# Token projections: the inverse norms go onto a diagonal that TensorE multiplies by

## The chip, the core and the metric

The program runs on one core of a Trainium2 chip. The metric is the device time of one execution in microseconds, as the median of three runs. TensorE (PE in the rows) does the matmuls, with PEld for its weight loads; VectorE is DVE, ScalarE is ACT, GpSimd is POOL and SyncE is SP.

## The reference, cut to what matters

The reference is two model blocks of two layers each, in float32. Every layer ends its mixer and its feed-forward part with the same step: a projection from a wide activation to the 1024 model columns, a root-mean-square norm over these columns, and a gated addition to the residual. Cut down, with `hidden` tokens by features:

```
m = hidden @ w_down                                   # (tokens, 1024)
n = m * rsqrt(mean(m * m, axis=-1) + 1e-6)            # one factor per token
h = h + n * gain                                      # gain: one factor per model column
```

There are 256 context tokens and 256 latent tokens in the first layer of the first block, 256 latent tokens after it.

## The kernel before, in words

The residual `h` and nearly all activations lie with model columns on the partitions (eight tiles of 128 columns, `KT`) and tokens along the free dimension (`S` = 256 for one half). Eight projections are computed the other way round, by the class `TokenProjection` (L897): 128 tokens on the partitions, 512 model columns in a bank. Each handles 256 tokens by 1024 columns as a two by two block scheme with seven products instead of eight (L971, `product`), all products in float32. The seven bank sums are combined by VectorE (`combine`, L1040) into four quarters `y[:, q]` of 128 tokens by 512 columns: q = 0 and 1 are the two column halves of tokens 0 to 127 (half 0), q = 2 and 3 those of tokens 128 to 255 (half 1).

Because tokens are on the partitions, the norm is one number per partition. ScalarE squares each quarter with a running sum along the row (L1029) and takes the root (L1034); VectorE takes the reciprocal (L1065). Half 1 is ready first. Then the quarters are scaled in place by the reciprocals: 2, 3 and 0 by VectorE (L1068), 1 by ScalarE (L1036). TensorE turns the scaled quarters back (`turn`, L1010): for half 1 and then half 0, eight transposes of 128x128 against the identity, from `y` into two banks' halves. VectorE adds them to the residual with the gain (`residual`, L1070, one instruction per k, L1075), waiting for the transposes of a pair of k in half 0.

The eight projections stand in these places:

- Projection A and projection B, the two token halves of the first layer's down projection (`WideDown`, L1181). B's products are interleaved with the end of A: A's transposes are in four groups, each between products of B (L1225). B's own transposes come after eight key products of `ContextKeys` (L1117).
- The output projections of the second layer of block one and of both layers of block two, and the down projections of the same three layers. `run` (L1077) issues products, then all 16 transposes. After five of the seven projections other than A (B, and those whose tails are at 1202, 1433, 1585 and 1991 us) `modulated_norm` (L555) follows: ScalarE squares each residual tile (L484), TensorE sums by a product with ones (L502), ScalarE takes the root (L489), VectorE the reciprocal (L510) and the normed tiles (L566). After the other two (1804 and 2211 us) a projection by the gate matrix follows directly on the residual tiles (L414).

The order of work on each engine is that of the program text: each stage adds its part to the queue of each engine, and the parts run in the order in which they were added, with semaphores between engines (`hit` names a count, `need` waits for it). Weights come through a ring of five chunks that SyncE's queue refills (L3051) when the products that read a chunk are done. Nothing plans or reorders. `K.root` is a scratch tile of two rows of 512 columns; its row 0 is used by the norms, its row 1 for a running sum of squares in other stages.

Of the kernel before, what the change touches and what calls it, by code (L numbers as in the profile page):

```python
# [16 lines left out]
ALU = mybir.AluOpType  # L17
ACT = mybir.ActivationFunctionType
AX = mybir.AxisListType.X

P = 128
D = 1024
KT = D // P
# [263 lines left out]
def need(eng, deps):  # L287

    for sig, count in deps:
        if count > 0:  # L290
            eng.wait_ge(sig.sem, count)
# [170 lines left out]


def scale_stage(K, groups, T, lhs, scale, apply, deps, eps="eps", n_apply=None, src_ready=None, sums=None):


# [8 lines left out]
    def scalar(act):  # L475
        need(act, deps)
        i = 0 if sums is None else 1
        for g, tiles in enumerate(groups):
            for t, src in enumerate(tiles if sums is None else []):
                if src_ready:  # L480
                    need(act, src_ready(t))
                if i >= n_square:
                    act.wait_ge(summed.sem, su + i - n_square + 1)
                act.activation(square[:, i % n_square, 0:T], src, ACT.Square).then_inc(squared.sem, 1)  # L484
                i += 1
            act.wait_ge(summed.sem, su + i)
            if g >= 2:
                act.wait_ge(applied.sem, ap + (g - 1) * (n_apply or len(groups)) // len(groups))
            act.activation(K.root[:, g % 2, 0:T], K.bank(4 + g % 2, T), ACT.Sqrt, bias=K.c(eps), scale=scale).then_inc(rooted.sem, 1)  # L489
# [119 lines left out]
class Modulation:  # L609
# [30 lines left out]
    def turn(self, pe):  # L640
        need(pe, self.after(1))
        for m in range(4):
            mm = pe.transpose(self.K.bank(self.banks[1])[:, m * P:m * P + P], self.row[:, m * P:m * P + P], self.K.c("ident"))
        mm.then_inc(self.sig[2].sem, 1)
# [9 lines left out]
def first_norm(K, h, piece, gains, gain, shift, out, tokens_ready, rest_of_constants):  # L654
# [17 lines left out]
    def scalar(act):  # L672
        need(act, tokens_ready)
        for k in range(KT):
            act.activation(out[:, k, :], h[:, k, :], ACT.Square).then_inc(sg["squared"].sem, 1)
        act.wait_ge(sg["summed"].sem, at["summed"] + 1)
        act.activation(r, K.bank(5), ACT.Sqrt, bias=K.c("eps"), scale=1.0 / D).then_inc(sg["rooted"].sem, 1)
        piece.keep(act)
        rest_of_constants(act)
        act.wait_ge(sg["n_gains"].sem, at["n_gains"] + 1)  # L680
        for k in range(1, KT, 2):
            act.wait_ge(sg["n_unit"].sem, at["n_unit"] + k + 1)
            for x, scale, bias in halves(k):
                ins = act.activation(x, x, ACT.Identity, bias=bias, scale=scale)
            ins.then_inc(sg["n_by_scalar"].sem, 1)
# [45 lines left out]
def attention_stage(K, rounds, outs, deps, buf, beside=None):  # L731
# [28 lines left out]
    def tensor(pe):  # L760
# [48 lines left out]
        for r in range(len(rounds) + 2):  # L809
            if r < len(rounds):  # L810
                score(r)
            if 1 <= r <= len(rounds):
                turn(r - 1)
                spread_inverse(r - 1)
            if r >= 2:
                weigh(r - 2)
# [80 lines left out]
class TokenProjection:  # L897
# [27 lines left out]
            K.next_blocks(CB, (self.sg["f_products"], self.at["f_products"] + (p + 1 if p < n - 2 else n + 5)))  # L925

    def reserve_tail(self):
        counts = {"squared": 4, "summed": 1, "rooted": 2, "row_inverses": 2, "taken_out_by_vector": 3, "taken_out_by_scalar": 1, "turned": KT, "applied": KT}
        self.sg.update({c: self.K.counter(c) for c in counts})
        self.at.update({c: self.sg[c].reserve(x) for c, x in counts.items()})  # L930

# [76 lines left out]
            self.product(pe, n - 1, i).then_inc(self.sg["f_products"].sem, 1)  # L1008

    def turn(self, pe, tiles):  # L1010
        scaled = {2: ("taken_out_by_vector", 1), 3: ("taken_out_by_vector", 2), 0: ("taken_out_by_vector", 3), 1: ("taken_out_by_scalar", 1)}
        for half in (1, 0):
            for k in tiles:
                if k % 4 == 0 or k == tiles[0]:
                    need(pe, [self.hit(*scaled[2 * half + k // 4])])
                mm = pe.transpose(self.tile(k)[:, half * P:half * P + P], self.y[:, 2 * half + k // 4, k % 4 * P:k % 4 * P + P], self.K.c("ident"))
                if not half:
                    mm.then_inc(self.sg["turned"].sem, 1)

    def norm(self, act):  # L1020
        sg, y = self.sg, self.y
        sums, partial, root, inverse = self.K.token_sum, self.K.token_partial, self.K.token_root[:, 0:2], self.K.token_inverse[:, 0:2]
        need(act, [self.final(1)])
        act.activation(y[:, 0], self.bank[1], ACT.Copy).then_inc(sg["f_first"].sem, 1)  # L1024
        for j, q in enumerate((0, 3, 2, 1)):
            need(act, [self.hit("f_quarters", j + 1)])
            if j == 2:
                need(act, [self.hit("squared", 1)])
            act.activation(self.junk[:, j % 2], y[:, q], ACT.Square, accum_out=sums[:, q:q + 1]).then_inc(sg["squared"].sem, 1)  # L1029
            if j >= 2:  # L1030
                half = 3 - j
                need(act, [self.hit("summed", 1)])
                need(act, [self.hit("squared", j + 1)])
                act.activation(root[:, half:half + 1], sums[:, q:q + 1], ACT.Sqrt, bias=partial[:, half:half + 1], scale=1.0 / D).then_inc(sg["rooted"].sem, 1)  # L1034
        need(act, [self.hit("row_inverses", 2)])
        act.activation(y[:, 1], y[:, 1], ACT.Copy, scale=inverse[:, 0:1]).then_inc(sg["taken_out_by_scalar"].sem, 1)  # L1036

    def combine(self, dve):
        sg, y, bank = self.sg, self.y, self.bank
# [19 lines left out]
    def scale(self, dve):  # L1059
        sg, y = self.sg, self.y  # L1060
        root, inverse = self.K.token_root[:, 0:2], self.K.token_inverse[:, 0:2]
        for half in (1, 0):
            iv = inverse[:, half:half + 1]
            need(dve, [self.hit("rooted", 2 - half)])
            dve.reciprocal(iv, root[:, half:half + 1]).then_inc(sg["row_inverses"].sem, 1)  # L1065
            need(dve, [self.hit("row_inverses", 2 - half)])
            for q in (2, 3) if half else (0,):
                dve.tensor_scalar(y[:, q], y[:, q], iv, None, ALU.mult).then_inc(sg["taken_out_by_vector"].sem, 1)  # L1068

    def residual(self, dve, h, gain, tiles):  # L1070
        lo = self.half * S
# [783 lines left out]
def even_projections(K, R, u, k_ready, qkvT, gate, qd, kvd, kpe, ktok, vtok, pads, conv, narrow, low_squares):  # L1855
# [24 lines left out]
    def tensor(pe):  # L1880
# [66 lines left out]
        for f in range(NF - 1):  # L1947
            project(f)
            if f == 1:
                key_rows()  # L1950
            elif f == 2:
                cumulate()
            if 3 <= f <= 10:
                unit_sum(f - 3)
            if f == 14 or f == 15:
                turn(2 * f - 28)
                turn(2 * f - 27)
            if f == 15:
                low_rank(0)
                low_rank(1)  # L1960
            if f == 16:
                for i in range(4, 8):
                    turn(i)
# [1144 lines left out]
```

## Time and profile before

| | us |
|---|---|
| median of three runs | 2255.86 |
| lowest, highest | 2252.78, 2255.88 |
| profiled execution, own time | 2256.64 |
| its span, first to last instruction | 2254.8 |
| TensorE matmul busy | 2171.7 (96%) |
| VectorE busy | 1051.4 (47%) |
| ScalarE busy | 461.0 (20%) |

The span is what the trace covers; the own time has a little more around it. The mean granted TensorE clock is 0.99 of full speed. Shares of busy time are means over the whole program.

### The profile page before, as it was taken

Reading aid. Unit: us, or ns where it says so; the run is one execution under the profiler, and the core shown is the slowest. Engines: PE = TensorE matmul, PEld = TensorE weight load, DVE = VectorE, ACT = ScalarE, POOL = GpSimd, SP = SyncE. Lnnn points to the kernel's source line nnn. Section 1 sums busy time; section 2 is a strip of 40 time slices with the busy share of each in tenths; the row PEclk is TensorE's granted clock in tenths of the full one; section 3 lists DMA queues with packets and bytes.
Section 4 is the critical chain, followed back from the end, with each engine's and each line's share of the span. In section 5 each row is a group of like instructions: output and inputs, shape, how many; then the busy total and the mean of one; then the engine's idle time right before and its main releaser. Section 6 shows DMA issues by size and latency. Waiting matters only on the chain.

```text
span 2254.8 us, 33258 instructions
## 1 busy us (share of the span) xinstructions
PE 2171.7 (96%) x14252; PEld 1512.5 (67%) x14252; DVE 1051.4 (47%) x1884; ACT 461.0 (20%) x988; POOL 139.0 (6%) x148
## 2 busy tenths in 40 slices
PE   6999999899899999999998999999999999999998
PEld 3447878464588885457466885686785478768646
DVE  2665555461654456652344114585324428642443
ACT  2433211351200000022153000223210022311001
POOL 0004333000000000002100000002000000200000
PEclk9999999999899999999999999999999999999999
DMA  8221444402422223445103444333344443334442
GB/s 324 75 75 43 152 154 167 160 1 75 187 94 79 90 94 132 173 147 141 60 1 131 149 150 169 142 128 113 126 154 168 150 149 114 111 131 149 168 168 75
DMA packets 41088, 285.66 MB, mean 127 GB/s; under 512 B 4976, under 2 KB 6384, under 8 KB 7152
## 3 DMA queue, kind: packets, MB, share of 16 engines
q1 hardware_dynamic: 38768, 275.79, 33.6%
q0 software_dynamic: 1312, 3.15, 1.1%
q10 hardware_dynamic: 864, 4.61, 0.5%
q8 instruction: 114, 1.87, 0.3%
q14 instruction: 30, 0.25, 0.0%
HBM read 281.95 MB, written 1.05 MB: 126 GB/s over the span
## 4 chain that ended last, share of the span: by engine, by line
PE 92%; DVE 4%; ACT 2%; issue 1%; DMA 1%; SPq 0%; ACTq 0%; DVEq 0%
PE banks L987 20%; PE banks L414 18%; PE banks L1398 12%; PE banks L1297 7%; PE banks L2552 6%; PE banks L1894 5%; PE banks L1577 2%; PE banks L1601 2%; PE banks L630 2%; PE banks L770 2%; PE banks L1597 1%; PE banks L502 1%; PE banks L2546 1%; PE banks L452 1%; PE banks L785 1%
## 5 line engine op out<-in xcount | busy, mean ns | idle before, releaser
L414 PE MATMUL banks<-normed,weight_ring 128*128 128x256 f32 (+1 forms) x1280 | 294.7, 393 | 7.8 <-DVE normed L566 5.7
L414 PEld LDWEIGHTS banks<-normed,weight_ring 128*128 128x128 f32 x1280 | 244.9, 192 | 56.9 <-issue 15.3
L987 PE MATMUL banks<-arena 128*128 128x512 f32 x360 | 171.0, 593 | 0.7 <-DVE arena L1453 0.5
L1297 PE MATMUL banks<-normed,weight_ring 128*128 128x256 f32 x704 | 153.9, 382 | 3.4 <-ACT normed L580 3.4
L1297 PEld LDWEIGHTS banks<-normed,weight_ring 128*128 128x128 f32 x704 | 134.8, 192 | 22.5 <-ACT normed L580 3.8
L987 PE MATMUL banks<-weight_ring,arena 128*128 128x512 f32 x322 | 149.2, 592 | 0.0
L2552 PE MATMUL banks<-normed,weight_ring 128*128 128x256 f32 x576 | 127.5, 381 | 5.8 <-DVE normed L566 2.9
L987 PEld LDWEIGHTS banks<-arena 128*128 128x128 f32 x360 | 68.2, 190 | 87.4 <-issue 86.1
L1894 PE MATMUL banks<-normed,weight_ring 128*128 128x512 f32 x288 | 126.1, 593 | 0.0
L2552 PEld LDWEIGHTS banks<-normed,weight_ring 128*128 128x128 f32 x576 | 108.6, 190 | 22.7 <-issue 5.0
L987 PEld LDWEIGHTS banks<-weight_ring,arena 128*128 128x128 f32 x322 | 60.9, 190 | 73.1 <-issue 72.9
L3014 DVE TENSOR_TENSOR arena<-arena 128x256 f32<-128x256 f32 x64 | 27.2, 425 | 171.1 <-ACT arena L3002 170.3
L952 DVE TENSOR_TENSOR arena<-weight_ring 128x512 f32<-128x512 f32 x59 | 40.7, 690 | 141.1 <-PE banks L987 141.1
L1894 PEld LDWEIGHTS banks<-normed,weight_ring 128*128 128x128 f32 x288 | 54.3, 190 | 66.7 <-issue 66.7
L1398 PE MATMUL banks<-normed,weight_ring 128*128 128x256 f32 x352 | 83.9, 393 | 6.7 <-ACT normed L580 4.3
L1398 PEld LDWEIGHTS banks<-normed,weight_ring 128*128 128x128 f32 x352 | 68.8, 197 | 19.0 <-issue 5.1
L1450 DVE TENSOR_TENSOR arena<-squares,banks 128x512 f32<-128x512 f32 x22 | 15.1, 687 | 132.1 <-ACT squares L1426 132.1
L1024 ACT ACTIVATE branch<-banks 128x512 f32<-128x512 f32 x8 | 4.8, 597 | 336.6 <-PE banks L987 336.6
L1315 DVE TENSOR_TENSOR arena<-banks,arena 128x256 f32<-128x256 f32 x22 | 9.3, 424 | 131.5 <-PE banks L1297 127.2
L630 PE MATMUL banks<-weight_ring,silu_cond 128*32 128x512 f32 x384 | 53.8, 649 | 14.2 <-ACT silu_cond L2860 7.1
L824 ACT ACTIVATE arena<-banks,attention_small 128x512 f32<-128x512 f32 (+2 forms) x96 | 54.0, 563 | 63.8 <-DVE attention_small L844 63.6
L3002 ACT ACTIVATE arena<-banks 128x256 f32<-128x256 f32 x64 | 24.5, 383 | 205.7 <-PE banks L414 205.7
(461 smaller groups left out, 3470.1 us busy)
## 6 DMA issues: line engine op xcount, KB each, us to landing
weight_ring<-in_weights SPq DMA_DIRECT2D x262, 1024.0 KB, 4.8
residual<-in_tokens ACTq DMA_DIRECT2D x1, 2048.0 KB, 12.7
mix<-in_rpb POOLq DMA_DIRECT2D x32, 64.0 KB, 3.6
constants<-in_const ACTq DMA_DIRECT2D x1, 1953.5 KB, 12.8
out<-residual SPq DMA_DIRECT2D x1, 1024.0 KB, 4.8
branch<-arena POOLq DMA_DIRECT2D x1, 512.0 KB, 4.9
normed<-in_ple POOLq DMA_DIRECT2D x1, 512.0 KB, 3.6
vector_params<-in_vectors ACTq DMA_DIRECT2D x1, 223.0 KB, 5.8
```

The costliest lines, as they stand in the source:

```text
L414: mm = pe.matmul(K.psum[lo:hi, banks[m % nb], 0:T], K.block(first[m] + k)[:, lo:hi], rhs(k), start=(k == 0), stop=(k == n_k - 1))
L630: mm = pe.matmul(o, self.silu[:, k, :], self.K.block(self.first[k] + 4 * j, 4), start=(k == 0), stop=(k == KT - 1))
L770: mm[j] = pe.matmul(ps[j], x.q(j), x.k(j), start=True, stop=x.bias is None)
L824: act.activation(prob[:, i % 4, 0:x.n], K.bank(i % 4, x.n), ACT.Exp, bias=maximum[:, i % 4:i % 4 + 1], accum_out=total[:, i % 4:i % 4 + 1] ...
L952: dve.tensor_tensor(out=t3, in0=b22, in1=b12, op=ALU.subtract)
L987: return pe.matmul(self.bank[i], left, b, start=(p == 0), stop=(p == n - 1))
L1297: mm = pe.matmul(K.bank(i % 4, T), K.block(first[i] + k), u[:, k, 0:T], start=(k == 0), stop=(k == KT - 1))
L1398: mm = pe.matmul(self.outs(p)[i], a[:, k * P:k * P + P], right(k), start=(k == 0), stop=(k == H - 1))
L1577: mm = pe.matmul(heads(2 * u)[halves[n], m, :], L[u][lv % 2][halves[n], m, :], X[u][halves[n], m, :], start=True, stop=True)
L1601: mm = pe.matmul(heads(2 * u + 1)[halves[n], m, :], PR[u][halves[n], m, :], Y[u][halves[n], m, :], start=True, stop=True)
L1894: mm = pe.matmul(K.bank(f % 4), K.block(first[f] + k), u[:, k, :], start=(k == 0), stop=(k == KT - 1))
L2552: mm = pe.matmul(K.bank(m % 2, S), K.block(first[m] + k), u[:, k, 0:S], start=(k == 0), stop=(k == KT - 1))
```

## The change

The quarters are no longer scaled. Instead VectorE scales the 128x128 identity by the inverse norms of a half (one factor per partition), which makes a diagonal matrix in row 1 of `K.root`, one for each half. TensorE then multiplies each 128x128 block of a quarter by that diagonal in an ordinary float32 product, where before it transposed the block against the identity. ScalarE's scaling and its semaphore are gone, and TensorE waits once per half for the diagonal instead of once per quarter.

```diff
     def turn(self, pe, tiles):
-        scaled = {2: ("taken_out_by_vector", 1), 3: ("taken_out_by_vector", 2), 0: ("taken_out_by_vector", 3), 1: ("taken_out_by_scalar", 1)}
+
         for half in (1, 0):
+            need(pe, [self.hit("taken_out_by_vector", 2 - half)])
             for k in tiles:
-                if k % 4 == 0 or k == tiles[0]:
-                    need(pe, [self.hit(*scaled[2 * half + k // 4])])
-                mm = pe.transpose(self.tile(k)[:, half * P:half * P + P], self.y[:, 2 * half + k // 4, k % 4 * P:k % 4 * P + P], self.K.c("ident"))
+                mm = pe.matmul(self.tile(k)[:, half * P:half * P + P], self.y[:, 2 * half + k // 4, k % 4 * P:k % 4 * P + P], self.diagonal(half), start=True, stop=True)
                 if not half:
                     mm.then_inc(self.sg["turned"].sem, 1)
+
+    def diagonal(self, half):
+        return self.K.root[:, 1, half * P:half * P + P]
...
-        need(act, [self.hit("row_inverses", 2)])
-        act.activation(y[:, 1], y[:, 1], ACT.Copy, scale=inverse[:, 0:1]).then_inc(sg["taken_out_by_scalar"].sem, 1)
...
             need(dve, [self.hit("row_inverses", 2 - half)])
-            for q in (2, 3) if half else (0,):
-                dve.tensor_scalar(y[:, q], y[:, q], iv, None, ALU.mult).then_inc(sg["taken_out_by_vector"].sem, 1)
+            dve.tensor_scalar(self.diagonal(half), self.K.c("ident"), iv, None, ALU.mult).then_inc(sg["taken_out_by_vector"].sem, 1)
```

The counters in `reserve_tail` change with it (`taken_out_by_vector` counts two instead of three).

## Rows read from the trace of the kernel before

**Rows 1.** The page: busy time, shares of the chain, a costly group.
```profile
PE 2171.7 (96%) x14252; PEld 1512.5 (67%) x14252; DVE 1051.4 (47%) x1884; ACT 461.0 (20%) x988; POOL 139.0 (6%) x148
...
PE 92%; DVE 4%; ACT 2%; issue 1%; DMA 1%; SPq 0%; ACTq 0%; DVEq 0%
...
L952 DVE TENSOR_TENSOR arena<-weight_ring 128x512 f32<-128x512 f32 x59 | 40.7, 690 | 141.1 <-PE banks L987 141.1
```
**Rows 2.** The changed lines: count, duration ns min/median/max; last, who waited (us, times).
```profile
L1016 PE MATMUL banks<-constants,branch x128: 272/273/332, 944.5 to 2213.0; 128*128 128x128 f32 x128
...
L1036 ACT ACTIVATE branch<-branch,token_roots x8: 722/722/724, 938.0 to 2211.6; 128x512 f32<-128x512 f32 x8
...
L1068 DVE TENSOR_SCALAR branch<-branch,token_roots x24: 478/486/489, 937.0 to 2211.6; 128x512 f32<-128x512 f32 x24
...
  PE banks L1016: 9.3, 12
```
**Rows 3.** Timeline, projection A: start us, us, engine line op, idle before.
```profile
938.04 0.72 ACT L1036 ACTIVATE branch<-branch,token_roots 128x512 f32<-128x512 f32 x1 [5.27 <-DVE token_roots L1065]
```
**Rows 4.** Chain that ended last, projection A: start us, us, what.
```profile
944.63 0.44 PE banks L1016 x4
```
**Rows 5.** Timeline of TensorE, projection B and the two stages behind it.
```profile
1002.09 3.62 PE L1117 MATMUL banks<-normed,weight_ring 128*128 128x256 f32 x16
...
1005.54 1.91 PE L1016 MATMUL banks<-constants,branch 128*128 128x128 f32 x16
1007.82 3.72 PE L502 MATMUL banks<-squares,constants 128*128 128x256 f32 x16 [0.37 <-ACT squares L484]
1011.38 3.73 PE L1124 MATMUL banks<-weight_ring,normed 128*128 128x128 f32 x32
```
**Rows 6.** Timeline, the norm tail at 1202, and TensorE's restart at 1443.
```profile
1201.64 0.88 DVE L1068 TENSOR_SCALAR branch<-branch,token_roots 128x512 f32<-128x512 f32 x2
...
1202.18 1.09 PE L1016 MATMUL banks<-constants,branch 128*128 128x128 f32 x8 [1.38 <-DVE branch L1068]
...
1202.91 0.49 DVE L1068 TENSOR_SCALAR branch<-branch,token_roots 128x512 f32<-128x512 f32 x1
...
1203.45 1.09 PE L1016 MATMUL banks<-constants,branch 128*128 128x128 f32 x8 [0.18 <-DVE branch L1068]
1203.93 3.23 DVE L1075 SCALAR_TENSOR_TENSOR residual<-banks,gains,residual 128x256 f32<-128x256 f32 x8 [0.53 <-PE banks L1016]
...
1204.92 3.72 PE L502 MATMUL banks<-squares,constants 128*128 128x256 f32 x16 [0.38 <-ACT squares L484]
...
1212.05 1.37 PE L1297 MATMUL banks<-normed,weight_ring 128*128 128x256 f32 x3 [3.41 <-ACT normed L580]
...
1442.79 0.89 PE L2552 MATMUL banks<-normed,weight_ring 128*128 128x256 f32 x3 [2.92 <-DVE normed L566]
```
**Rows 7.** Timeline, the direct tail at 2211.
```profile
2210.36 0.88 DVE L1068 TENSOR_SCALAR branch<-branch,token_roots 128x512 f32<-128x512 f32 x2
...
2213.19 12.14 PE L414 MATMUL banks<-residual,weight_ring 128*128 128x256 f32 x55
```
**Rows 8.** Lines with operations like the added ones: duration ns min/median/max.
```profile
L1124 PE MATMUL banks<-weight_ring,normed x64: 272/275/275, 1011.4 to 1037.0; 128*128 128x128 f32 x64
...
L2764 DVE TENSOR_SCALAR arena<-arena x4: 227/260/293, 1520.1 to 1939.0; 128x128 f32<-128x128 f32 x2, 128x256 f32<-128x256 f32 x2
...
L1055 DVE TENSOR_SCALAR token_roots<-token_roots x8: 160/160/163, 929.8 to 2208.5; 128x2 f32<-128x2 f32 x8
```
**Rows 9.** Stretches: us, busy per engine, then PEclk, DMA share, GB/s.
```profile
1202.00:1205.00 3.00, 2.27 (x17) 1.80 (x17) 2.24 (x7) 1.86 (x6) 0.00 (x0) 1.00 0.80 336
1212.00:1216.00 4.00, 3.95 (x10) 3.15 (x11) 3.83 (x12) 2.79 (x7) 0.00 (x0) 0.57 0.00 0
...
2001.00:2005.00 4.00, 3.94 (x11) 3.21 (x12) 2.78 (x8) 0.00 (x0) 0.00 (x0) 0.59 0.00 0
1443.00:1447.00 4.00, 4.00 (x20) 3.48 (x20) 2.46 (x7) 0.38 (x1) 0.00 (x0) 1.00 0.00 0
```

More of the change, by code:

```diff
@@ L927, in reserve_tail @@
     def reserve_tail(self):
-        counts = {"squared": 4, "summed": 1, "rooted": 2, "row_inverses": 2, "taken_out_by_vector": 3, "taken_out_by_scalar": 1, "turned": KT, "applied": KT}
+        counts = {"squared": 4, "summed": 1, "rooted": 2, "row_inverses": 2, "taken_out_by_vector": 2, "turned": KT, "applied": KT}
         self.sg.update({c: self.K.counter(c) for c in counts})
```

## The prediction

> **What bounds the kernel now.** I read the page's busy shares and its chain first [rows 1]. TensorE is busy 96% of the span and its matmuls carry 92% of the chain that ended last, so a microsecond of matmul counts fully unless TensorE was waiting there anyway. Then I listed the instructions of the lines that change [rows 2]: 128 transposes, which is 16 in each of eight token projections, 24 quarter scalings on the vector engine, eight on the scalar engine and 16 reciprocals. TensorE's matmuls waited for the scalings 9.3 us in all, twelve times, which is 1.38 + 0.18 us in each of six tails [rows 2, 6]. So there is little waiting to win back. Last I read the tails in order of time, because the transposes sit in four different surroundings [rows 3 to 7].
>
> - Projection A (the first of the wide down projection): its transposes stand in four groups of four between products of projection B. TensorE goes from L987 to L1016 to L987 with no gap, each group taking 0.44 us of the chain [rows 4]. The last scaling was done at 938.04 + 0.72 = 938.8, almost 6 us before the first transpose [rows 3, 4].
> - Projection B: eight key products (L1117, 16 records) cover the whole norm chain. The 16 transposes then run as one block of 1.91 us, and L502 follows as soon as the first square of the residual is there [rows 5].
> - Four tails (at 1202, 1433, 1585 and 1991 us) that are followed by a norm: TensorE waits for the scaled quarters, twice, then for squares, and L502 runs 16 records back to back [rows 6].
> - Two tails (at 1804 and 2211) that are followed directly by the gate product L414, which is dense from its first product on [rows 7].
>
> **What the change does to each operation.** Removed: four scalings of 128x512 per projection, 0.486 us on VectorE (three) and 0.722 on ScalarE (one) [rows 2]. Added: two scalings of the 128x128 identity on VectorE. The nearest row is a tensor-scalar of 128x128 elsewhere, 0.227 us (the shortest of that line; two of its four are 128x128, two 128x256) [rows 8]. Bounds: 0.160 us for 128x2 [rows 8] and 0.486 for 128x512 [rows 2]. I take 0.227. The reciprocals stay.
>
> Replaced: 128 transposes by 128 full f32 products of the same shape. This is the dear part. The trace of before has a full f32 product with 128 moving columns in L1124: the code has 32 of them (two calls, two token tiles, eight k each) and the trace has 64 matmul records, so each product is two records, as are the key products of L1117 (16 records for eight) [rows 5, 8]. A transpose is one record (128 for 128). Pace: 32 records of L1124 take 3.73 us, of which 0.275 is the last one's own length, (3.73 - 0.275)/31 = 0.1115 us per record [rows 5, 8]. The 16 transposes of projection B take 1.91 us, (1.91 - 0.273)/15 = 0.109 [rows 2, 5], the pace of the tails too (0.273 + 7 x 0.109 = 1.04 for eight), and there the granted clock is 1.00, that is 2.4 GHz [rows 9]. So 16 transposes cost 1.75 us of TensorE and 16 products cost 32 x 0.1115 = 3.57: 1.82 us more per projection. The lower bound of the pace is the transposes' 0.109 per record; no row suggests an upper one for this form.
>
> **Sum by place.** Two small constants from the rows: a block after a wait loses 0.05 us at its start (eight transposes take 1.09 after a wait instead of 1.04), and L502 after a wait takes 3.72 where 16 records of the same shape without one (L1117) take 3.62, so 0.10 [rows 5, 6].
>
> A: nothing hides TensorE's time there, so +1.82. VectorE is itself behind TensorE in this stage (L952 waits for L987 for 141 us in all [rows 1]), so its 1.5 us of saved scaling buys nothing.
>
> B: the saved scalings lie under the eight key products, again nothing. Products run 1005.54 to 1009.11. The first square waits for the fourth record of half 0 instead of the second: (16 + 4) x 0.1115 against (8 + 2) x 0.109 is +1.14, so it is released at about 1008.96, before TensorE is free. L502 starts at 1009.11 instead of 1007.82, without its 0.10 start loss: +1.19.
>
> Each of the four norm tails, by the numbers of 1202 [rows 6]: the scaling of half 1 starts at 1201.64 and the transposes at 1202.18, so 0.486 plus 0.055 of signalling. With the diagonal the products start at 1201.64 + 0.227 + 0.055 = 1201.92, which is 0.26 earlier. Half 1 then holds TensorE for 0.05 + 16 x 0.1115 until 1203.75. The diagonal of half 0 is ready at 1202.91 + 0.227 + 0.055 = 1203.19, so it is no longer waited for: what was TensorE's wait for VectorE becomes VectorE's wait for TensorE. Half 0 ends at 1205.54. The first residual starts at 1203.75 + 3 x 0.1115 + 0.275 + 0.04 = 1204.40 instead of 1203.93, its square releases L502 at 1204.92 + 0.47 = 1205.39, and TensorE is free only at 1205.54. L502 starts 0.62 later and saves its 0.10: +0.52, and four times that is 2.08. The residuals step by (3.23 - 0.48)/7 = 0.39 us per k, L502 by two records of 0.216, so TensorE sets L502's end and the square root, reciprocal and norm behind it move by the same 0.52.
>
> Each of the two direct tails, by 2211 [rows 7]: products from 2210.36 + 0.282 = 2210.64, done at 2210.64 + 0.05 + 3.57 = 2214.26. L414 starts then instead of at 2213.19, less the 0.10: +0.97. The residuals, 0.39 apart as above and from about 2213.1, stay ahead of L414, whose k takes 0.43. Two of them: 1.94. The scalar engine's table load that stood behind its scaling comes earlier and is of no use to anyone.
>
> Total: 1.82 + 1.19 + 2.08 + 1.94 = 7.0 us. The profiled execution took 2256.64 us (span 2254.8), 0.8 above the median of 2255.86, so its own time becomes 2263.7 and the median 2262.9. With the diagonal at 0.160 the six waiting tails each gain 0.07 (-0.4), at 0.486 they lose 0.26 (+1.6); with 0.109 per record, 256 records give -0.6. So 6.0 to 8.6 without the clock. DMA queues aren't touched: weights are released by the products before, and a later TensorE only gives the loads more time.
>
> **A rule against the trace.** Behind three of the norm tails (1202, 1585, 1991) TensorE's clock was granted at half (1.2 GHz) for a stretch, after TensorE had stood idle in the norm (3.41 us at 1212); of the three windows of 4 us around these the first reads 0.57 and the last 0.59, against 1.00 at 1443, though there too TensorE had been idle 2.92 us [rows 6, 9]. Each costs some 4 x 0.42 = 1.7 us, together 5.0. The stretch with the transposes themselves is at 1.00 [rows 9]. The Trainium skill, "TensorE: Matmul & The Clock Gate", Part 4, says that transpose mode does not count as engine activity for the clock as a matmul does. By that rule real products in the tail could keep the clock up; the rows put the idle time in the norm, behind the transposes, where this change adds no work, so I take none of it in the sum and keep it as a rival. The same page's Terms say that transpose mode is 4x faster for FP32; the rows say two records against one, nearly 2x. By that rule the change would cost several times the sum above; that is rival 3.
>
> **The rivals.**
> 1. The clock moves: which of the idle times in the norms are followed by a half-clock stretch comes out otherwise. Gives back: all three half-clock stretches go, 2262.9 - 5.0 = 2257.9. Takes: the 1433 tail and one more get a stretch too, 2262.9 + 3.4 = 2266.3. For: the tail at 1433 has nearly the idle time of 1202 and no loss, and the three runs of before lie 3.1 us apart, two such stretches. Against: the idle times behind the tails keep their length. Chances 0.07 and 0.07 for a change of two or more; one more or fewer (2261.2, 2264.6) is inside the forecast.
> 2. The other side: the product with a diagonal is a single record at transpose pace. Then half 1 is done by 1202.84, half 0 starts when its diagonal is ready at 1203.19 instead of 1203.45, and each waiting tail gains 0.26: -1.6 in six, A and B unchanged, 2254.3. It decides at one record per product; the record counts of L1124 and L1117 speak against [rows 5, 8]. Not slower. Chance 0.06.
> 3. The product is four records at the transposes' pace, 4 x 0.109 = 0.436 us, 6.98 for 16: 3.41 us more than in my sum for each of eight projections, 27.3, so 2290.2. L1124 speaks against. Chance 0.02.
>
> **How the numbers follow.** Forecast (two records a product, clock within one stretch) 0.76: 2262.9, own range 2260.5 to 2265. Rivals 0.22 as above, 0.02 for the unforeseen. 0.2% is 4.5 us, about what this measurement can tell from no change: slower means above 2260.4, faster below 2251.3. Slower 0.81 (the forecast almost whole, the clock's taking, rival 3), same 0.15 (clock giving back, the single record, the low edge of the forecast), faster 0.04 (single record with luck at the clock). The range 2259.0 to 2267.0 leaves out the single record and the far tails.
>
> **What would show it.** Right: 256 matmul records on the line that had 128 transposes, 0.11 apart; VectorE's two diagonals near 0.23 us; in the tail at about 1206 no gap on TensorE between half 1 and half 0; L502 following the products without a wait; L414 at 2214 plus the shift so far, about 1 us later behind the last scaling. The A groups take 0.89 instead of 0.44 us of the chain. Wrong: 128 records, or a gap between the halves, or half-clock stretches that come or go in number by more than one.

## The result

| | before | after |
|---|---|---|
| median us | 2255.86 | 2271.04 |
| lowest, highest of five | 2251.91, 2258.53 | 2263.19, 2272.14 |
| profiled execution, own time | 2256.64 | 2272.14 |
| its span | 2254.8 | 2270.3 |
| mean granted TensorE clock | 0.990 | 0.987 |

The changed kernel is slower: ratio 1.0055, 95% interval [1.0039, 1.0071], which is 12.4 us; the medians of five differ by 15.2. The forecast had the direction, and its 2262.9 us and its upper end of 2267.0 are too low.

The page of the kernel after, first lines of parts 1, 4 and 5. It answers to [rows 1].
```profile
PE 2189.4 (96%) x14380; PEld 1533.4 (68%) x14380; DVE 1045.3 (46%) x1876; ACT 455.5 (20%) x980; POOL 139.0 (6%) x148
...
PE 92%; DVE 5%; ACT 2%; issue 1%; DMA 1%; SPq 0%; DVEq 0%; ACTq 0%
...
L952 DVE TENSOR_TENSOR arena<-weight_ring 128x512 f32<-128x512 f32 x59 | 40.7, 690 | 141.9 <-PE banks L987 141.9
```
TensorE has 128 records more (14380 for 14252) and is as busy in share. VectorE and ScalarE have each lost some 6 us of work, nearly all of which nobody waited for: VectorE's L952 waits for TensorE as long as before.

The two changed lines in the kernel after (durations in ns, least, median, most; the last line says how long TensorE's products waited for the diagonal). They answer to [rows 2].
```profile
L1015 PE MATMUL banks<-roots,branch x256: 272/275/377, 942.7 to 2228.6; 128*128 128x128 f32 x128
...
L1067 DVE TENSOR_SCALAR roots<-constants,token_roots x16: 285/288/292, 935.3 to 2226.0; 128x128 f32<-128x128 f32 x16
...
  PE banks L1015: 7.1, 6
```
There are 256 records where there were 128. Waits are six, not twelve: only half 1 waits. The diagonal takes 0.288 us, not 0.227.

Projection A in the chain that ended last, against [rows 4]: 0.89 us a group for 0.44.
```profile
948.04 0.89 PE banks L1015 x8
```
TensorE around projection B, in order of time, against [rows 5]: 3.73 us where 1.91 stood, and L502 follows without a wait.
```profile
1002.12 3.62 PE L1116 MATMUL banks<-normed,weight_ring 128*128 128x256 f32 x16
1005.57 3.73 PE L1015 MATMUL banks<-roots,branch 128*128 128x128 f32 x32
1009.14 3.62 PE L502 MATMUL banks<-squares,constants 128*128 128x256 f32 x16
```
The first norm tail after, in order of time, against [rows 6].
```profile
1202.91 0.29 DVE L1067 TENSOR_SCALAR roots<-constants,token_roots 128x128 f32<-128x128 f32 x1
...
1203.25 3.84 PE L1015 MATMUL banks<-roots,branch 128*128 128x128 f32 x32 [1.17 <-DVE roots L1067]
...
1204.18 0.29 DVE L1067 TENSOR_SCALAR roots<-constants,token_roots 128x128 f32<-128x128 f32 x1
1205.79 3.23 DVE L1074 SCALAR_TENSOR_TENSOR residual<-banks,gains,residual 128x256 f32<-128x256 f32 x8 [1.32 <-PE banks L1015]
...
1206.93 3.62 PE L502 MATMUL banks<-squares,constants 128*128 128x256 f32 x16
```
The wait before half 1 is 0.2 us shorter (1.17 for 1.38) and the one between the halves is gone: 32 records in one block. But the block lasts 3.84 us, the residual waits 1.32 us for it instead of 0.53, and from the scaling's start to L502 it is 4.02 us instead of 3.28.

The last direct tail after, against [rows 7].
```profile
2224.74 0.29 DVE L1067 TENSOR_SCALAR roots<-constants,token_roots 128x128 f32<-128x128 f32 x1
2225.07 3.65 PEld L1015 LDWEIGHTS banks<-roots,branch 128*128 128x128 f32 x32 [2.00 <-DVE roots L1067]
...
2228.75 4.48 PE L414 MATMUL banks<-residual,weight_ring 128*128 128x256 f32 x20
```
L414 stands 4.01 us behind the start of the scaling instead of 2.83.

So the tails go as forecast, within 0.2 us each. Where are the other microseconds? Stretches of the kernel after; the third number from the end is the granted clock. They answer to [rows 9].
```profile
1446.00:1450.00 4.00, 4.00 (x13) 3.17 (x12) 2.02 (x6) 0.00 (x0) 0.00 (x0) 0.58 0.02 4
1463.00:1471.00 8.00, 8.00 (x29) 6.87 (x30) 7.68 (x19) 0.20 (x1) 0.00 (x0) 0.57 0.26 109
1549.00:1556.00 7.00, 7.00 (x39) 5.06 (x36) 2.10 (x9) 2.91 (x15) 6.61 (x8) 0.51 0.49 206
1607.00:1611.00 4.00, 4.00 (x12) 3.20 (x11) 1.73 (x5) 0.00 (x0) 0.00 (x0) 0.57 0.00 0
2013.00:2020.00 7.00, 5.96 (x14) 4.80 (x15) 3.72 (x9) 0.00 (x0) 0.00 (x0) 0.52 0.00 0
1214.00:1218.00 4.00, 4.00 (x11) 3.18 (x12) 3.83 (x12) 2.71 (x7) 0.00 (x0) 0.57 0.00 0
```
The same places in the kernel before.
```profile
1446.00:1450.00 4.00, 4.00 (x21) 3.51 (x20) 0.00 (x0) 0.41 (x2) 0.00 (x0) 1.00 0.00 0
1460.00:1466.00 6.00, 6.00 (x30) 5.33 (x30) 5.79 (x14) 0.58 (x2) 0.00 (x0) 1.00 0.31 102
1543.00:1550.00 7.00, 7.00 (x59) 4.95 (x60) 2.95 (x12) 4.42 (x22) 6.69 (x8) 1.00 0.25 103
```
Length times what is missing to 1.00 gives 1.7 + 3.4 + 3.4 + 1.7 + 3.4 + 1.7 = 15.3 us in the kernel after. In the kernel before, the three stretches known from the prediction (1212, 1594, 2001) give 5.0. (Each trace has one more behind the last projection, of about 1.7 us.) All six in the kernel after follow a spot where TensorE idles or does little: the norm gaps (1214, 1446, 1607, 2013; TensorE idle 2.87 to 3.41 us), the 16-column products of the sparse layer (1463) and the idle 1.45 us before its attention (1549). "Weak spot" stands for such a place from here on. A stretch is called single where it takes about 1.7 us and doubled where it takes 3.4.

What the change touches lies between the first transposes of projection A and the start of the last L414. From the one to the other the profiled execution of before takes 1268.7 us and that of after 1286.1: 17.3 more, of which 15.3 - 5.0 = 10.3 is this difference in half clock, and 7.0 is left, the size of the forecast sum. (A little too much is counted as half clock: of the stretch at 2013, TensorE idled 1.04 us.) The whole executions differ by only 15.5 us, because in this one execution the kernel after was 1.8 us ahead when it reached projection A. Up to there TensorE has the same products in both kernels, and the half-clock stretches of the first 600 us fall differently in each trace.

### The profile page after: what moved, and what is told of

It is laid out like the page before. It is cut to its first block, busy times and chain, and to the rows that moved or that the text cites. A ratio compares the mean times of both kernels' runs of the same rounds, so it can differ in the third digit from the quotient of the medians.

```text
span 2270.3 us, 33498 instructions
## 1 busy us (share of the span) xinstructions
PE 2189.4 (96%) x14380; PEld 1533.4 (68%) x14380; DVE 1045.3 (46%) x1876; ACT 455.5 (20%) x980; POOL 139.0 (6%) x148
## 4 chain that ended last, share of the span: by engine, by line
PE 92%; DVE 5%; ACT 2%; issue 1%; DMA 1%; SPq 0%; DVEq 0%; ACTq 0%
PE banks L987 20%; PE banks L414 18%; PE banks L1397 12%; PE banks L1296 7%; PE banks L2551 6%; PE banks L1893 5%; PE banks L1576 2%; PE banks L1600 2%; PE banks L770 1%; PE banks L630 1%; PE banks L1596 1%; PE banks L1015 1%; PE banks L2545 1%; PE banks L452 1%; PE banks L785 1%; PE banks L776 1%
## 5 line engine op out<-in xcount | busy, mean ns | idle before, releaser
L414 PE MATMUL banks<-normed,weight_ring 128*128 128x256 f32 (+1 forms) x1280 | 296.2, 394 | 7.8 <-DVE normed L566 5.7
L414 PEld LDWEIGHTS banks<-normed,weight_ring 128*128 128x128 f32 x1280 | 245.9, 193 | 57.4 <-issue 15.3
L1296 PE MATMUL banks<-normed,weight_ring 128*128 128x256 f32 x704 | 153.9, 382 | 3.4 <-ACT normed L580 3.4
L2551 PE MATMUL banks<-normed,weight_ring 128*128 128x256 f32 x576 | 131.9, 390 | 5.8 <-issue 2.9
L952 DVE TENSOR_TENSOR arena<-weight_ring 128x512 f32<-128x512 f32 x59 | 40.7, 690 | 141.9 <-PE banks L987 141.9
L1397 PE MATMUL banks<-normed,weight_ring 128*128 128x256 f32 x352 | 84.6, 396 | 6.5 <-ACT normed L580 4.3
L844 DVE TENSOR_REDUCE attention_small<-banks 128x1 f32<-128x512 f32 (+2 forms) x96 | 48.4, 531 | 41.0 <-PE banks L776 36.3
```

Of the source, the lines that this page charges most:

```text
L414: mm = pe.matmul(K.psum[lo:hi, banks[m % nb], 0:T], K.block(first[m] + k)[:, lo:hi], rhs(k), start=(k == 0), stop=(k == n_k - 1))
L844: dve.reduce_max(maximum[:, i % 4:i % 4 + 1], K.bank(i % 4, rounds[r].n), AX, negate=True).then_inc(sg["maxima"].sem, 1)
L952: dve.tensor_tensor(out=t3, in0=b22, in1=b12, op=ALU.subtract)
L1296: mm = pe.matmul(K.bank(i % 4, T), K.block(first[i] + k), u[:, k, 0:T], start=(k == 0), stop=(k == KT - 1))
L1397: mm = pe.matmul(self.outs(p)[i], a[:, k * P:k * P + P], right(k), start=(k == 0), stop=(k == H - 1))
L2551: mm = pe.matmul(K.bank(m % 2, S), K.block(first[m] + k), u[:, k, 0:S], start=(k == 0), stop=(k == KT - 1))
```

## The experiments

All are timed against the kernel before on the same chip; diffs are against that kernel unless said. Stretches are given by when they start.

**The same two kernels again.** No edit.

> The kernel before once more, nothing edited. Two theories on why the change cost 15.2 us by the medians (12.6 by the ratio) where its tails were worked out at 7.0. Luck: TensorE's half-clock stretches fall differently in each execution whatever the kernel is, the fixed cost is 7 to 9 us, and this kernel against itself scatters by up to 6 us between runs (2251.9 to 2258.5 so far). Cause: the change itself brings more half-clock time. Both expect a ratio of 1.000 here within 0.15%; the trace's half-clock time tells how far it scatters with no change (44 us at half clock in the first trace of before, 58 in the one of after).

> The changed kernel once more. Fixed cost alone: 7 to 9 us above the kernel before, ratio 1.003 to 1.004, and half-clock time in its trace within what the kernel before shows. If the change causes half-clock time: 13 to 16 us again, ratio 1.0055 to 1.007, and half-clock time above the kernel before's in every trace.

Measured: before against itself 1.0009 [0.9995, 1.0024], runs from 2251.6 to 2267.8 us; after 1.0061 [1.0043, 1.0079], median 2269.84 against 2257.32. The difference is systematic, 12.5 us by the medians and more than the fixed cost (what the change costs with the clock left aside), so "luck in one execution" falls. But executions of equal mean granted clock differ by much less. Means over all executions of the two kernels up to the eighth experiment: at 0.988 the kernel before takes 2264.2 (six executions) and after 2269.8 (two), at 0.989 2263.1 (one) and 2271.3 (two), at 0.990 2260.7 (five) and 2265.2 (four), which is 4.5 to 8.2 us. The mean clock is 0.991 before and 0.9885 after. The new trace of after shows the same doubled stretches (1461, 1547, 2011); the new trace of before the same three (1213, 1595, 2001). From projection A to the last L414 the new traces take 1267.4 and 1284.4 us, 17.0 apart, and here the kernel after was 4.4 us ahead at projection A. Over all executions (0.986 to 0.990 for the kernel after; its two traces have 0.987 and 0.988) the difference is only 12 to 13 us. If both kernels reach projection A at the same time on average, some 5 us of half clock come on top of the fixed cost in a middle execution, and the 10 of these two traces are more than usual.

**Products without the rest of the change.**
```diff
-                mm = pe.transpose(self.tile(k)[...], self.y[...], self.K.c("ident"))
+                mm = pe.matmul(self.tile(k)[...], self.y[...], self.K.c("ident"), start=True, stop=True)
```

> Scalings kept as before, only the transposes become full products with the identity. By the sum's rows: A +1.8, B +1.2, each of four norm tails +0.78 (no earlier start: 0.52 + 0.26), each of two direct tails +1.23, together +8.6 us, ratio 1.0038, with the clock aside. If a product were one record it would be 0. If the scaling's removal was what hurt, this kernel would be no slower than before. In the trace: 256 matmul records 0.11 us apart on the line that had 128.

Measured: 1.0065 [1.0054, 1.0077], median 2271.16 against 2257.32, +13.8 us. The tail at 1203 in its timeline: VectorE's scaling of half 1, TensorE's block, L502.
```profile
1203.64 0.88 DVE L1068 TENSOR_SCALAR branch<-branch,token_roots 128x512 f32<-128x512 f32 x2
...
1204.18 3.84 PE L1016 MATMUL banks<-constants,branch 128*128 128x128 f32 x32 [1.37 <-DVE branch L1068]
1207.85 2.32 PE L502 MATMUL banks<-squares,constants 128*128 128x256 f32 x10
```
From the scaling to L502 it is 4.21 us (4.02 in the kernel after, 3.28 before). The products alone carry the whole cost, and the diagonal and the lighter VectorE give back 0.2 us in a waiting tail. Two records a product, 3.84 us for 32. Here too the time is some 5 us above the fixed sum of 8.6, with single stretches at 1447 and 1856 that before lacks and a doubled one at 2010. In the trace the two parts can be told apart: from projection A to the last L414 it takes 1282.4 us, 13.7 more than the kernel before, with 10.2 us of half clock behind 1200 us instead of 5.0. That leaves 8.5 for the products, and 8.6 was expected.

**Scalings left out, nothing in their place.** Transposes stay, and the residual gets unscaled values.
```diff
...
-        need(act, [self.hit("row_inverses", 2)])
-        act.activation(y[:, 1], y[:, 1], ACT.Copy, scale=inverse[:, 0:1])...
-            for q in (2, 3) if half else (0,):
-                dve.tensor_scalar(y[:, q], y[:, q], iv, None, ALU.mult)...
...
         for half in (1, 0):
+            need(pe, [self.hit("row_inverses", 2 - half)])
             for k in tiles:
-                if k % 4 == 0 or k == tiles[0]:
-                    need(pe, [self.hit(*scaled[2 * half + k // 4])])
```

> Transposes as before, the four scalings of 512 columns left out with nothing in their place (the residual gets unscaled values), and TensorE waits for the reciprocals alone. This is the most that a free way of scaling could bring: the transposes of half 0 start at reciprocal + 0.05 instead of + 0.54, so 0.5 us earlier in each of six waiting tails, A and B unchanged: -3.1 us, ratio 0.9986. If waiting for the scalings were worth more than the profile shows (a rival), it would be 6 us or more.

Measured: 1.0019 [1.0007, 1.0031], median 2262.03: four to five us slower, against both expectations, although it does less work and has no product. The place of its transposes was as expected: in the trace each waiting tail starts 0.52 us earlier (TensorE waits 0.85 us there instead of 1.38), half 1 right behind the reciprocal.
```profile
1196.19 0.16 DVE L1061 RECIPROCAL token_roots<-token_roots 128x1 f32<-128x1 f32 x1
...
1196.40 1.09 PE L1014 MATMUL banks<-constants,branch 128*128 128x128 f32 x8 [0.85 <-DVE token_roots L1061]
```
Its clock in three stretches of the second sparse layer tells the rest.
```profile
1842.00:1849.00 7.00, 5.64 (x13) 4.54 (x14) 4.00 (x9) 0.00 (x0) 0.00 (x0) 0.54 0.00 0
1863.00:1870.00 7.00, 7.00 (x22) 5.90 (x22) 6.71 (x16) 0.20 (x1) 0.00 (x0) 0.51 0.23 95
1948.00:1955.00 7.00, 7.00 (x38) 5.10 (x38) 2.38 (x10) 2.93 (x15) 6.61 (x8) 0.53 0.52 219
```
From projection A to the last L414 it takes 1273.4 us, 4.7 more than before, with 15.3 us of half clock behind 1200 us where before has 5.0. So it doesn't take products in the tail to make the clock fall: a kernel whose tails are 0.52 us shorter each loses more clock, and so does one whose tails are longer.

**TensorE kept at work in the weak spots, in both kernels.** Three products that serve nothing after an L502 sum (`fill` is 3 there), three among the 16-column products of each sparse layer, two before each sparse attention; none before 1200 us. The expectations speak of four L502 sums; the edit reaches five, for the norm behind the gate product of the tail at 1804 has one too (30 records on the added line, from 1206 to 2001 us).
```diff
+        for _ in range(fill):
+            pe.matmul(K.bank(5), K.c("ones"), K.const[:, 0:512], start=True, stop=True)
...
+                        if name == "wi" and k % 4 == 3 and (t, k) != (1, 7):
+                            pe.matmul(K.bank(3), K.c("ones"), K.const[:, 0:512], start=True, stop=True)
...
         rotate(7)
+        for _ in range(2):
+            pe.matmul(K.bank(6), K.c("ones"), K.const[:, 0:512], start=True, stop=True)
```

> The kernel before with products that serve nothing where TensorE idles or does little behind the tails: three after each of the four L502 sums, three among the 16-column products of each sparse layer, two before each sparse attention. They cost some 2 x 3 x 0.86 = 5.1 us plus the part of 2 x 1.7 us that the idle time of 1.45 us does not hold (0.5), and should take away the half-clock stretches behind 1200 us: about 5 us more than the kernel before, less 1.7 us for each stretch that goes (three to four in its traces), so 2256 to 2259 in all. Both theories (places of the stretches moved by the change; stretches made by the products) expect the same here; this is one half of a pair.

> The changed kernel with the same filling products. If the change's cost is its fixed 7.4 us (A 1.8, B 1.2, norm tails 4 x 0.54, direct tails 2 x 1.1) plus half-clock stretches in places that the filling closes, this kernel is 7.4 us above fill_before (6.5 to 8.5) although the unfilled pair differs by 12 to 13. If something else of the change costs the other 5 us (products that hold back TensorE later, DMA, a slower engine), the pair differs by 12 to 13 again.

Measured: fill_before 0.9997 [0.9985, 1.0010], median 2256.23; fill_after 1.0033 [1.0021, 1.0045], median 2265.48. The pair differs by 0.0036, 8.1 us (9.3 by the medians); the unfilled pair, same_after against same_before, by 0.0052, 11.7 us (12.0 by the medians). Each ratio has an interval of 0.0012 to 0.0018 to either side, so by the times alone the drop is hardly clear of the noise, and the traces have to carry it. Neither filled trace has a half-clock stretch between 1200 us and the last L414. Spots of above in fill_after, all at full clock.
```profile
1448.00:1452.00 4.00, 4.00 (x20) 3.53 (x19) 2.09 (x6) 0.38 (x1) 0.00 (x0) 1.00 0.00 0
1462.00:1470.00 8.00, 8.00 (x45) 6.28 (x45) 7.66 (x18) 0.20 (x1) 0.00 (x0) 1.00 0.37 133
1548.00:1556.00 8.00, 8.00 (x66) 5.78 (x68) 3.39 (x15) 4.22 (x22) 7.61 (x9) 1.00 0.50 211
```
With the clock out of the way the fixed cost can be read off two traces. TensorE in fill_before, the first transposes of projection A and the last direct tail:
```profile
942.54 0.60 PE L1018 MATMUL banks<-constants,branch 128*128 128x128 f32 x4
...
2212.03 4.15 PE L414 MATMUL banks<-residual,weight_ring 128*128 128x256 f32 x18
```
and in fill_after:
```profile
946.46 1.05 PE L1017 MATMUL banks<-roots,branch 128*128 128x128 f32 x8
...
2223.82 4.48 PE L414 MATMUL banks<-residual,weight_ring 128*128 128x256 f32 x20
```
From the one to the other it is 1269.49 us and 1277.36: 7.9 us, of which 0.1 is given back behind L414's start. Between these two points each trace has one half-clock stretch, both single (at 1111 and 1119 us).

**Less work, with the clock held.** no_scaling with the same filling products.

> no_scaling with the same filling products as fill_before (the residual gets unscaled values). Unfilled, leaving the scalings out saved 0.52 us in each of six waiting tails and yet measured 4 us slower, with 60 us at half clock in its trace. If the half-clock stretches are what hid the gain, this kernel is 3.1 us below fill_before (2253 against 2256). If leaving work out costs time in some other way, it is 4 us above fill_before.

Measured: 0.9982 [0.9973, 0.9990], median 2254.11. That is 0.0015, 3.4 us, below fill_before (2.1 by the medians), and 3.1 was the sum of its six tails. The times alone would leave room for less; the trace does not. Projection A and the last direct tail in it:
```profile
942.94 0.60 PE L1016 MATMUL banks<-constants,branch 128*128 128x128 f32 x4
...
2209.26 3.94 PE L414 MATMUL banks<-residual,weight_ring 128*128 128x256 f32 x17
```
That is 1266.32 us, 3.2 less than in fill_before, again with a single stretch at half clock (1112). Unfilled the same edit was 4 to 5 us slower than before. This settles the sign of that experiment: the half clock hid the gain.

**A pure delay.** Two products that serve nothing, once, in projection B's stage.
```diff
                 need(pe, [hit("squared", k + 1)])
+                for _ in range(0 if k else 2):
+                    pe.matmul(K.bank(3), K.c("ones"), K.const[:, 0:512], start=True, stop=True)
```

> The kernel before with two products that serve nothing (four records, 1.7 us) once, in projection B's stage before the sums on bank 3; all else as before. If the half-clock stretches depend on where later idle times fall and not on what the tails do, the time does not move by 1.7 but by 1.7 plus a change in half-clock time of up to 5 us either way, and the trace shows other stretches than in the kernel before. If only the diagonal products cause them: +1.7 (ratio 1.0008), stretches at the same stages as before (1212, 1595, 2001).

Measured: 1.0002 [0.9990, 1.0014], median 2258.01; the expected 1.7 us cannot be told from nothing by the times. In the trace it is there: from projection A to the last L414 it takes 1269.1 us where same_before, whose half-clock time between these points is the same, takes 1267.4. Its stretches behind it begin at 1213, 1595 and 2001, as before. That is against the first theory as I had put it: this one delay, ahead of all weak spots, did not set other spots off. The four kernels that do show other stretches (after, product_only, no_scaling, split_scaling) all change each tail, and so the distance from one weak spot to the next. That this distance is what counts is a guess; no run changes it by itself.

**A split scaling**, as a version that could beat the kernel before.
```diff
+                if not half and k == 2:
+                    need(pe, [self.hit("taken_out_by_vector", 4)])
...
-            for q in (2, 3) if half else (0,):
-                dve.tensor_scalar(y[:, q], y[:, q], iv, None, ALU.mult)...
+            for t in (y[:, 2], y[:, 3]) if half else (y[:, 0, 0:2 * P], y[:, 0, 2 * P:]):
+                dve.tensor_scalar(t, t, iv, None, ALU.mult)...
```

> A version of the kernel before that may beat it: the scaling of quarter 0 is cut in two instructions of 256 columns, so that the first transposes of half 0 start after 0.29 us of scaling instead of 0.49: first residual and L502 or L414 0.2 us earlier in each of six waiting tails, -1.2 us in all (ratio 0.9995), nothing in A and B. Against: the second piece must be done before the third transpose (0.2 us later), else the gain is smaller. Half-clock stretches moving can cover it in the median; the trace shows it per tail.

Measured: 1.0015 [1.0002, 1.0029], median 2262.24, slower. The tail itself gained 0.14 us, from the first scaling to the residual 2.15 us instead of 2.29:
```profile
1202.10 0.88 DVE L1070 TENSOR_SCALAR branch<-branch,token_roots 128x512 f32<-128x512 f32 x2
...
1204.25 2.05 DVE L1077 SCALAR_TENSOR_TENSOR residual<-banks,gains,residual 128x256 f32<-128x256 f32 x5 [0.27 <-PE banks L1018]
```
and the clock lost it many times over, behind three of the weak spots that cost the kernel after:
```profile
1442.00:1449.00 7.00, 6.02 (x14) 4.88 (x15) 3.62 (x9) 0.00 (x0) 0.00 (x0) 0.52 0.00 1
1462.00:1470.00 8.00, 8.00 (x29) 6.83 (x29) 7.68 (x19) 0.20 (x1) 0.00 (x0) 0.57 0.27 115
1548.00:1555.00 7.00, 7.00 (x39) 5.13 (x36) 2.05 (x9) 2.88 (x15) 6.61 (x8) 0.51 0.48 199
```

**Filling only where it is nearly free**, without and with the split scaling. The diff is the filling's without its middle piece.

> The kernel before, with filling products only where TensorE idles anyway (three after each of four L502 sums, two before each sparse attention), none among the 16-column products. Their own cost is 2 x 0.3 us. If the half-clock stretches behind the norm tails (three of 3.4 us in each trace of before, 1.7 us of loss each) are real losses that follow from the idle time, they go and the kernel is 4 to 5 us faster than before (ratio 0.998). If the loss is only moved (a stretch at the 16-column products instead), it is 0 to 2 us.

> fill_idle_only with the split scaling of quarter 0: measured per tail in the trace at 0.14 us, so 0.8 us less than fill_idle_only, 5 to 6 us faster than the kernel before (ratio 0.9975). A version that may beat both.

Measured: fill_idle_only 0.9998 [0.9987, 1.0008], median 2256.38; fill_and_split 0.9988 [0.9977, 0.9999], median 2256.19. In fill_idle_only the stretches behind the norm gaps are gone, but they come back at the unfilled 16-column products:
```profile
1458.00:1462.00 4.00, 4.00 (x14) 3.38 (x14) 3.86 (x10) 0.20 (x1) 0.00 (x0) 0.57 0.26 109
1864.00:1871.00 7.00, 7.00 (x23) 5.83 (x23) 6.71 (x16) 0.20 (x1) 0.00 (x0) 0.52 0.22 94
1211.00:1215.00 4.00, 3.16 (x16) 2.72 (x16) 3.90 (x12) 3.31 (x8) 0.00 (x0) 1.00 0.00 0
```
5.1 us of loss there against the 5.0 of the norm gaps: moved, not removed, the second of the two outcomes named. fill_and_split is the one version that beats both kernels, by 2.7 us (1.1 by the medians) where 5 to 6 were expected, and hardly clear of the noise.

## Why the prediction was wrong

1. Two records a product at 0.11 us, the dear part: right. 256 records; A 0.89 for 0.44 a group, +1.8 us in all as computed; B +1.2 (L502 at 3.57 behind the block's start instead of 2.28, less 0.1). Rivals 2 and 3, one record or four, are refuted by the record count and the pace (32 records in 3.73 us).
2. A and B hide nothing, and VectorE's saved time is worth nothing there: right.
3. The norm tails: +0.74 from scaling to L502, less the 0.10 of L502's start, is 0.64 where 0.52 was forecast. The diagonal took 0.288 us and not 0.227 (+0.06), and a block of 32 records loses 0.11 us after a wait and not 0.05 (3.84 against 3.73). The wait between the halves went and the residual waits for TensorE, as forecast.
4. The direct tails: 4.01 - 2.83 - 0.10 = 1.08 for 0.97, by the same two terms.
5. The sum: 1.8 + 1.2 + 4 x 0.64 + 2 x 1.08 = 7.7 us by these rows and 7.8 of fixed cost read off the filled pair, where the forecast said 7.0 and its bounds 6.0 to 8.6. Right, but for the 0.7 to 0.8 of points 3 and 4.
6. What failed is the step "so I take none of it in the sum", with rival 1 at a chance of 0.07 for each side. The granted clock was treated as chance with an even hand. It isn't: behind 1200 us and up to the last L414 both traces of before have three single stretches, 5.0 us, and both traces of after six spots with three of the stretches doubled, 15.3 us. Over all executions the kernel after is 12 to 13 us slower (15.2 in the first five), of which 7.8 are fixed and, by what is left, some 5 are half clock; with the weak spots filled, 8 to 9 are left. What happened is the "takes" side of rival 1, and its price (two more stretches, 3.4 us) was too low as well, because a stretch at half clock was taken as always single. The trace of before already had longer ones ahead of the change, 34 to 45 and 591 to 602 us at a granted clock of 0.53. The argument "the idle times keep their length" was true of the norms (2.92 us before the restart at 1446, 3.41 at 1214, as before) and did not help.
7. The transposes of the tail at 1202 ran at a granted clock of 1.00 in the kernel before, and so did the products of the same tail in the kernel after (1203 to 1207 us). The clock rule of the Trainium skill, "TensorE: Matmul & The Clock Gate", Part 4, that transposes do not count as activity, would have made real products help the clock. The runs show more half clock with them, and as much of it with transposes in shorter tails (no_scaling 15.3 us behind 1200 us; split_scaling 13.6); nothing here shows that transposes and products count differently. The section "HAM oscillation — how this bites in real kernels" of the same page of the Trainium skill describes a kernel that falls back to the low clock at one idle gap after the other. The trace of after agrees in part: at five of its six spots behind 1200 us TensorE had idled 1.45 to 3.41 us, at the sixth it was busy with 16-column products.

Left open: what decides that a weak spot is followed by a half-clock stretch, and how long it lasts; and so why this change brings more of them than the kernel before has. That the extra time is half clock is shown by the traces; why the change causes it is not.

## What to carry to other kernels

Turning by a product with a diagonal saves scalings but doubles TensorE's records in float32: where TensorE is the bound, and the scaling engines have time, it loses, and the saved wait (0.2 us a tail here) is a tenth of what the records cost (1.8 us). When a kernel has idle or thin spots on TensorE, an edit of half a microsecond per stage, longer or shorter, can bring half-clock stretches worth several microseconds; so compare kernels at equal granted clock, or with the weak spots filled in both, before a small edit is judged. Filling gave no clear gain here: with all weak spots closed, the filling products cost as much as the clock gave back (fill_before 0.9997), and with the 16-column products left unfilled the half clock moved there (fill_idle_only 0.9998).

## What the runs showed that was not expected

- Leaving work out made the kernel slower: 2262.0 us against 2257.3 without the scalings, and 2254.1 once the weak spots were filled in the same kernel.
- A half-clock stretch can last 7 us and more: windows of 7 us at 0.51 to 0.52 in the kernel after, where before had only single ones behind 1200 us. The one at 2013 doubled though dense products (L414) followed the gap.
- Thirty-two products of 16 columns, TensorE busy all the time by its records, can be followed by half clock just as an idle time is (1458 and 1864 us in fill_idle_only, 0.57 and 0.52).
- Scaling 128x128 values by a per-partition value takes VectorE 0.288 us where the tensor-scalar of the same shape at L2764 takes 0.227. That one has two constants of the instruction for scalars and other operations; which of the differences counts was not tried.
